# Two attention stages of a fused transformer kernel moved into the projection loop ahead of them

## The chip, the cores and the metric

The kernel runs on one core of one Trainium2 chip. The metric is the device time of one execution in microseconds; the median of several executions counts. Five engines work side by side and meet at semaphores: TensorE (PE, matrix products; PEld is its weight load), VectorE (DVE), ScalarE (ACT), GpSimd (POOL) and SyncE (SP). Here SP issues the weight loads and POOL a few small ones.

## The reference, cut to what matters

Two transformer blocks on 256 tokens of width 2048, all in float32. The change lies in the first block, between its first projection and its gated linear attention:

```
mod  = silu(c) @ w_ada + b_ada            # six rows of 2048, wanted later
h    = rms_norm(x) * (1 + scale1) + shift1
proj = h @ w_in                           # 7680 columns of q, k, v, r, then 16 of a, then the gates
o_sb  = stick_breaking_attention(rms_norm(q_sb), rms_norm(k_sb), v_sb)      # 6 heads of 128
o_dil = dilated_mixture(rms_norm(q_dil), rms_norm(k_dil), v_dil)            # 2 slots of 3 heads of 128
o_gla = gla_chunked(q_gla, k_gla, v_gla, log_sigmoid(a @ w_gla_a + b) / 16) # 4 heads
y = g0 * (o_sb @ w_br_sb) + g1 * (o_dil @ w_br_dil) + g2 * (o_gla @ w_br_gla)
```

A stick-breaking head needs, for 256 queries and keys: z = k q, softplus of z, its reverse running sum (a product with a triangle of -1), exp of z plus that sum under a strict causal mask, and the product with v. A dilated slot takes one softmax over the logits of three heads with a fixed bias each, and sums their products with v.

## The kernel before

**Products.** A weight tile of 256 x 512 (512 KB) lands in one of eight buffers `raw`. ACT copies it to `whi` in the rounded type float32r, DVE writes the rest of it to `wlo` (`split_item`, four buffers each), and PE makes 12 matmuls of 512 columns: high by high, low by high, high by low, for two halves of the tile and two blocks of tokens (`products`). Eight tiles make a group of 512 columns of `proj`; then ACT and DVE copy the two banks of the group to `proj1` (`proj1_evac`). The split of tile p + 4 waits for the product of tile p, so that up to three tiles lie ready when PE ends one.

**The stage of the first projection** (`ST_PROJ1`). The first three groups of columns are made while the modulation is computed. Then 96 tiles p = 0 to 95 follow in three rounds of 32, and between them 16 tiles of `w_ada` in each round, which DVE alone takes in (`ada_rows`, summed in `acc2`); at the end of each round PE turns that sum into columns (`ada_columns`). `BRANCH_ORDER` is the order of the 48 tiles of a round: four of the product, then one of `w_ada` and two of the product in turn. `drive` runs this order with an offset of four tiles. Behind the loop stands `side`, the 16 columns of a. The loads run up to eight tiles ahead of the splits; each waits until DVE has used up its buffer.

**Stages.** `stage_end` drains each of PE, ACT and DVE and makes them wait for each other. Behind the projection come the stage of the six stick-breaking heads (`ST_SB`), that of the dilated heads (`ST_DIL`) and that of the gated linear attention (`ST_GLA`). In the first two no weight tile is split or loaded beyond the eight that lie ready. `qk_norm` squares q and k of both kinds (ACT, `SQ1`), sums them, takes the root and multiplies. A head is a chain: PE turns q and k, DVE copies them out scaled (`qkt_evac`), PE makes z, ACT takes four functions of it, DVE adds and masks three times, PE makes the running sum, DVE adds and masks three times, ACT takes the exponential, PE multiplies with v, ACT and DVE copy out high and low part. Two heads are under way at once, in pairs of banks. POOL fetches the constants of each stage when the stage before it has ended (`wait_stage`).

Of the kernel before, what the change touches and what calls it, by code (L numbers as in the profile page):

```python
# [12 lines left out]
P = 128  # L13
# [83 lines left out]
def program(nc, I, out):  # L97
    ctx = ExitStack()
    with ctx:
# [15 lines left out]
        alo = sb("alo", [P, DC, TB * P], F32R)  # L115
        bhi = sb("bhi", [P, DC, TB * P], F32R)
# [5 lines left out]
        def pair_tile(t):  # L122

            pair = raw[:, t % 8 - t % 2:t % 8 - t % 2 + 2].rearrange("p h a (b n) -> p h (a b) n", n=HID)
            return pair[:, :, 2 * (t % 2):2 * (t % 2) + 2].rearrange("p h k n -> p k h n")

# [47 lines left out]
        class Chain:  # L174
# [11 lines left out]
        (ST_LOAD, ST_PROJ1, ST_SB, ST_DIL, ST_GLA, ST_BRANCH, ST_OUT1, ST_FFN, ST_PROJ2, ST_FOX, ST_OUT2,  # L186
         ST_MOE) = range(1, 13)
# [101 lines left out]
        moe_pe, moe_act, moe_dve = S("moe_pe"), S("moe_act"), S("moe_dve")  # L289

# [169 lines left out]
        side_t = {1: region(xf, 1280, 256), 2: region(big, T2, 256), 3: region(big, 5376, 256)}  # L460
# [3 lines left out]
        def _(pool):  # L464
# [12 lines left out]
            wait_stage(pool, ST_DIL)  # L477
# [28 lines left out]
        acc2 = region(xf, 256, 2 * COLS)  # L506
# [123 lines left out]
        def _(pe):  # L630
# [53 lines left out]
            def side(n, no, bias=None):  # L684
# [10 lines left out]
                ins.then_inc(S("side_mm"), 1)  # L695
                pe.wait_ge(S("side_t"), no)
# [3 lines left out]
                ins.then_inc(S("side_done"), 1)  # L700

# [60 lines left out]
            def proj1_tile(k, g, par):  # L762
                is_product, j = BRANCH_ORDER[k]
                if is_product:
                    q = j // 8
                    if j % 8 == 0:
                        group_free(g * 4 + (n_proj1 + q))
                    products(t_proj1 + k, g * 6, [(ahi, alo, 2 * (j % 8)), (ahi, alo, 2 * (j % 8) + 1)],
                             (2 * (q % 2), 2 * (q % 2) + 1), j % 8 == 0, j % 8 == 7, j)

            def proj1_ada(g, par):
                ada_columns(g * 48 + (t_proj1 + 48), g + 4, acc2, 5)
            drive(pe, 3, 48, proj1_tile, {47: proj1_ada}, single=True)
            side(16, 1)
            stage_end(pe, "pe")


            H = SB_HEADS
            pe.wait_ge(S("qk_scaled"), 1)
            for i in range(H + 3):  # L780
                if i < H:
                    qk_transposes("sb", i, i)
                h = i - 1
                if 0 <= h < H:
                    pe.wait_ge(S("sb_qkt"), 2 * (h + 1))
                    if h >= 2:
                        pe.wait_ge(S("sb_sp"), h - 1)
                    q, k = qkt_sb[:, h % 2, 0], qkt_sb[:, h % 2, 1]
                    mm(bank[2 + h % 2][:, 0:256], k[:, 0:P], q[:, 0:256], start=True, stop=True)
                    mm(bank[2 + h % 2][:, 256:384], k[:, P:256], q[:, P:256], start=True, stop=True)\  # L790
                        .then_inc(S("sb_z"), 1)
                h = i - 2
                if 0 <= h < H:
                    pe.wait_ge(S("sb_spm"), h + 1)
                    if h >= 2:
                        pe.wait_ge(S("sb_e"), h - 1)
                    sp_, C = l_sb[:, h % 2], bank[4 + h % 2]
                    mm(C[:, 0:P], negtri, sp_[:, 0:P], start=True, stop=True)
                    mm(C[:, P:256], negtri, sp_[:, P:256], start=True, stop=False)
                    mm(C[:, P:256], negones, sp_[:, 256:384], start=False, stop=True)  # L800
                    mm(C[:, 256:384], negtri, sp_[:, 256:384], start=True, stop=True).then_inc(S("sb_c"), 1)
                h = i - 3
                if 0 <= h < H:
                    pe.wait_ge(S("sb_w"), h + 1)
                    if h >= 2:
                        pe.wait_ge(S("sb_out"), h - 1)
                    _, _, _, v = att_cols("sb", h)
                    W, O = z_sb[:, h % 2], bank[6 + h % 2]
                    mm(O[:, 0:P], proj1[:, 0, v:v + DH], W[:, 0:P], start=True, stop=True)
                    mm(O[:, P:256], proj1[:, 0, v:v + DH], W[:, P:256], start=True, stop=False)  # L810
                    mm(O[:, P:256], proj1[:, 1, v:v + DH], W[:, 256:384], start=False, stop=True).then_inc(S("sb_o"), 1)
            stage_end(pe, "pe")

            def pv(kind, u, i):
                a = ATT[kind]
                per, n = a["per"], u * a["per"] + i
                pe.wait_ge(S(att(kind) + "_pt"), HEAD0[kind] + n + 1)
                if i == 0 and u >= 2:
                    pe.wait_ge(S(att(kind) + "_out"), UNIT0[kind] + u - 1)
# [8 lines left out]
            def attention(kind):  # L828
# [6 lines left out]
                for n in range(U * per + 2):  # L835
                    if n + 1 < U * per:
                        qk_transposes(kind, a["head"](*divmod(n + 1, per)), n + 1)
# [1609 lines left out]
```

## Time and profile before

| | us |
|---|---|
| median of 3 runs | 3216.33 (3214.28 to 3217.31) |
| the profiled execution | 3211.53 |
| its span in the trace | 3209.8 |
| PE, DVE, ACT busy in the span | 2909.0, 1979.2, 1480.1 |

The tiles of the projection's loop run from about 160 to 424 us of the span, the stick-breaking stage from 431 to 510, the dilated one to 544, and the gated linear attention to about 655. Times in the trace are counted from the start of the span. A matmul is listed with its latency, and several overlap; what one costs in a row of them is the distance from start to start. PEclk is the share of full clock that TensorE was granted: 0.5 is 1.2 GHz and 1.0 is 2.4 GHz, and a value between is a mean over a stretch.

### The profile page before, as it was taken

The page shows a single profiled execution, that of the slowest core. Times are in us where ns is not written, and L with a number is a line of the kernel's source. Part 1 is how long each engine was busy: PE and PEld are TensorE (multiplying, and loading weights), DVE is VectorE, ACT ScalarE, POOL GpSimd, SP SyncE. Part 2 cuts the span into 40 slices and gives each one's busy share as a digit, 9 for nine tenths or more (in the row PEclk, how much of TensorE's full clock was granted, in tenths as well). Part 3 has the DMA queues.
Part 4 walks back from the last instruction along what each step waited for, and adds up shares of the span by engine and source line. Part 5 has one row for each costly group of instructions (what it writes and reads, how often), then busy time and mean ns, then how long its engine had stood idle before and what let it go on. Part 6 is the DMA issues. An engine that isn't in the chain of part 4 may idle for free.

```text
span 3209.8 us, 38239 instructions
## 1 busy us (share of the span) xinstructions
PE 2909.0 (91%) x12771; PEld 2358.5 (73%) x12771; DVE 1979.2 (62%) x2206; ACT 1480.1 (46%) x1757; POOL 13.0 (0%) x21
## 2 busy tenths in 40 slices
PE   3799955799999899999999989977779999999989
PEld 3688853378887678888888868855668887878767
DVE  7876653367777744554555554446664557989875
ACT  3344343244444444444434444434354436777763
POOL 0000000000000000000000000000000000000000
PEclk8899976599999999999999999976889999999999
DMA  9988830078887746665665657710425568999964
GB/s 339 339 284 283 283 102 19 2 244 277 288 283 268 237 151 189 191 193 186 190 196 182 197 142 194 193 51 14 135 83 189 185 197 303 371 351 356 365 243 142
DMA packets 347283, 676.76 MB, mean 211 GB/s; under 512 B 23800, under 2 KB 114320, under 8 KB 346656
## 3 DMA queue, kind: packets, MB, share of 16 engines
q1 hardware_dynamic: 345664, 669.29, 63.2%
q0 software_dynamic: 1504, 5.95, 0.6%
q8 instruction: 72, 1.18, 0.2%
q14 instruction: 43, 0.35, 0.0%
HBM read 673.04 MB, written 2.10 MB: 210 GB/s over the span
## 4 chain that ended last, share of the span: by engine, by line
PE 75%; DVE 5%; ACT 3%; issue 1%; DMA 1%; DVEq 0%; ACTq 0%; POOL 0%; SPq 0%; POOLq 0%
PE bank L641 23%; PE bank L643 23%; PE bank L642 23%; PE bank L845 1%; PE bank L918 1%; ACT big L1222 0%; PE bank L848 0%; PE bank L1091 0%; DVE alo L1709 0%; PE bank L922 0%; DVE big L2212 0%; ACT whi L1206 0%; PE bank L920 0%; DVE big L2177 0%; DVE wlo L1683 0%
## 5 line engine op out<-in xcount | busy, mean ns | idle before, releaser
L641 PE MATMUL bank<-whi,ahi 128*128 128x512 f32 x2400 | 944.6, 394 | 43.2 <-DVE wlo L1873 30.2
L1671 DVE TENSOR_TENSOR wlo<-raw,whi 128x1024 fp32r<-128x1024 f32 x540 | 653.7, 1224 | 483.3 <-ACT whi L1200 478.7
L642 PE MATMUL bank<-wlo,ahi 128*128 128x512 f32 x2400 | 939.7, 392 | 0.0
L643 PE MATMUL bank<-whi,alo 128*128 128x512 f32 x2400 | 939.6, 392 | 0.0
L1200 ACT ACTIVATE whi<-raw 128x1024 fp32r<-128x1024 f32 x540 | 567.5, 1059 | 580.1 <-PE bank L643 524.9
L641 PEld LDWEIGHTS bank<-whi,ahi 128*128 128x128 f32 x2400 | 454.4, 189 | 139.1 <-issue 29.5
L643 PEld LDWEIGHTS bank<-whi,alo 128*128 128x128 f32 x2400 | 453.9, 189 | 96.1
L642 PEld LDWEIGHTS bank<-wlo,ahi 128*128 128x128 f32 x2400 | 454.5, 189 | 93.5
L1193 ACT ACTIVATE whi<-raw 128x1024 fp32r<-128x1024 f32 x280 | 296.7, 1061 | 432.2 <-PE bank L643 372.3
L1873 DVE TENSOR_TENSOR wlo<-raw,whi 128x1024 fp32r<-128x1024 f32 x280 | 341.8, 1224 | 205.9 <-ACT whi L1193 203.2
L641 PE MATMUL bank<-whi,bhi 128*128 128x512 f32 x944 | 369.8, 392 | 32.6 <-DVE wlo L1671 32.6
L642 PE MATMUL bank<-wlo,bhi 128*128 128x512 f32 x944 | 368.4, 390 | 0.0
L643 PE MATMUL bank<-whi,blo 128*128 128x512 f32 x944 | 368.3, 390 | 0.0
L1683 DVE TENSOR_TENSOR wlo<-raw,whi 128x1024 fp32r<-128x1024 f32 x256 | 302.1, 1222 | 69.0 <-ACT whi L1206 66.6
L1206 ACT ACTIVATE whi<-raw 128x1024 fp32r<-128x1024 f32 x256 | 262.6, 1056 | 90.0 <-PE bank L643 71.9
L641 PEld LDWEIGHTS bank<-whi,bhi 128*128 128x128 f32 x944 | 177.8, 188 | 70.9 <-issue 33.0
L643 PEld LDWEIGHTS bank<-whi,blo 128*128 128x128 f32 x944 | 177.8, 188 | 37.2
L642 PEld LDWEIGHTS bank<-wlo,bhi 128*128 128x128 f32 x944 | 177.9, 188 | 36.7
L641 PE MATMUL bank<-whi,ghi 128*128 128x512 f32 x384 | 154.2, 402 | 3.2 <-DVE wlo L1683 2.8
L643 PE MATMUL bank<-whi,glo 128*128 128x512 f32 x384 | 150.0, 391 | 0.0
L642 PE MATMUL bank<-wlo,ghi 128*128 128x512 f32 x384 | 149.8, 390 | 0.0
L1828 DVE SCALAR_TENSOR_TENSOR xres<-raw,silu_c,xres 128x1024 f32<-128x1024 f32 x105 | 134.8, 1284 | 9.7 <-ACT big L1447 4.4
(441 smaller groups left out, 1892.6 us busy)
## 6 DMA issues: line engine op xcount, KB each, us to landing
raw<-in_w_in SPq DMA_DIRECT2D x296, 512.0 KB, 4.6
raw<-in_w_ada SPq DMA_DIRECT2D x192, 512.0 KB, 5.3
raw<-in_w_ffn_in SPq DMA_DIRECT2D x352, 256.0 KB, 3.3
raw<-in_w_expert_gate SPq DMA_DIRECT2D x128, 512.0 KB, 5.6
raw<-in_w_expert_up SPq DMA_DIRECT2D x128, 512.0 KB, 6.5
raw<-in_w_expert_down SPq DMA_DIRECT2D x128, 512.0 KB, 6.2
raw<-in_w_ffn_out SPq DMA_DIRECT2D x88, 512.0 KB, 4.3
raw<-in_w_out SPq DMA_DIRECT2D x64, 512.0 KB, 4.6
```

The costliest lines, as they stand in the source:

```text
L641: mm(o, shi[:, kc, T], whi[:, s, c], start=st, stop=False)
L642: mm(o, shi[:, kc, T], wlo[:, s, c], start=False, stop=False)
L643: ins = mm(o, slo[:, kc, T], whi[:, s, c], start=False, stop=en)
L845: ins = mm(Z[:, zs], q[:, qs], k[:, ks], start=True, stop=not fox)
L918: mm(O, gl_sc[rows, h * 2 + b, :], proj1[rows, b, v:v + DV], start=True, stop=(c == 0))
L1193: A(whi[:, u % 4], raw[:, t % 8], ACT.Copy).then_inc(hi_ready, 1)
L1200: A(whi[:, t % 4], raw[:, t % 8], ACT.Copy).then_inc(hi_ready, 1)
L1206: A(whi[:, t % 4].rearrange("p k (h n) -> p k h n", h=2), pair_tile(t), ACT.Copy).then_inc(hi_ready, 1)
L1671: V.tensor_tensor(wlo[:, t % 4], raw[:, t % 8], whi[:, t % 4].bitcast(F32), ALU.subtract)\
L1683: V.tensor_tensor(as_tile(wlo[:, t % 4]), pair_tile(t), as_tile(whi[:, t % 4].bitcast(F32)), ALU.subtract).then_inc(lo_ready, 1)
L1828: V.scalar_tensor_tensor(sums, w, col, sums, ALU.mult, ALU.add).then_inc(lo_ready, 1)
L1873: V.tensor_tensor(wlo[:, u % 4], raw[:, t % 8], whi[:, u % 4].bitcast(F32), ALU.subtract)\
```

## The change

The two stages `ST_SB` and `ST_DIL` are gone. Their work is cut into slots, one for each tile p of the projection (`sb_step(h)` = 8 + 4h, `dil_step(u, i)` = 48 + 2(3u + i)). PE does its part of slot p right behind the product of tile p. ACT and DVE do theirs in `proj1_slot(p)`, which stands ahead of the split of tile p + 4. The norm of q and k is split in two, at p = 0 to 5 for the stick-breaking heads and at p = 40 to 45 for the dilated ones. The heads now have one bank for each purpose (4 for turned q and k and the columns of `w_ada`, 5 for z, 6 for the running sum or turned probabilities, 7 for the output) instead of pairs. `side_products` stands ahead of tile 0, its transposes behind tile 1. The sum of the `w_ada` rows lies in `acc1`, over the buffer of the attention outputs. POOL fetches the constants of the first kind when the normed x is there and the biases of the second when all six heads are out. The loop over the three rounds is written out.

```diff
-            wait_stage(pool, ST_PROJ1)
+            pool.wait_ge(S("norm_xn"), 2)
             fetch("sbc_landed", region(xf, X_SBC, 3 * P), I["consts"][:, C_U:C_U + 3 * P])
-            wait_stage(pool, ST_SB)
+            pool.wait_ge(S("sb_out"), SB_HEADS)
             for j in range(2):
                 fetch("dmask_landed", proj1[:, j, 0:3 * 384], I["consts"][:, at:at + 3 * 384])
-            wait_stage(pool, ST_DIL)
+            wait_stage(pool, ST_PROJ1)
             fetch("glac_landed", region(xf, G_R, 448), I["consts"][:, C_R:C_R + 448])
...
# PE
+            def sb_pe(p):
+                for h in range(SB_HEADS):
+                    at = p - sb_step(h)
+                    if at == 0:   # waits qk_scaled 1, sb_qkt 2h;        4 transposes -> bank 4, sb_T
+                    elif at == 2: # waits sb_qkt 2(h + 1), sb_sp h;      z -> bank 5 (256 + 128 columns), sb_z
+                    elif at == 5: # waits sb_spm h + 1, sb_e h;          running sum -> bank 6 (4 x 128), sb_c
+                    elif at == 7: # waits sb_w h + 1, v's group, sb_out h; output -> bank 7 (3 x 128), sb_o
+            def dil_pe(p):        # head n: transposes at 0, logits at 2; past 11 + i turned
+                                  # probabilities (3 x 128), past 12 + i the product with v (3 x 128)
+            side_products(16, 1)
+            for it in range(3):
+                for k, (is_product, j) in enumerate(BRANCH_ORDER):
+                    products(...)
+                    if p == 1:
+                        side_flip(16, 1)
+                    sb_pe(p)
+                    dil_pe(p)
+                    if j == 31:
+                        ada_columns(t_proj1 + 48 * (it + 1), it + 4, acc1, 4)
...
# ACT
+                    if at == 2:
+                        act.wait_ge(S("sb_z"), h + 1)
+                        A(ZS, Z, ACT.Copy).then_inc(S("sb_zs"), 1)
+                        chain.step(A(L, Z, ACT.Abs))
+                        chain.step(A(L, L, ACT.Exp, scale=-1.0))
+                        A(L, L, ACT.Ln, bias=1.0).then_inc(S("sb_ln"), 1)
+                    elif at == 6:
+                        act.wait_ge(S("sb_e"), h + 1)
+                        act.wait_ge(S("sb_em"), h + 1)
+                        A(ZS, ZS, ACT.Exp).then_inc(S("sb_w"), 1)
+                    elif at == 7:
+                        act.wait_ge(S("sb_o"), h + 1)
+                        A(bhi[:, h, :], bank[7][:, 0:256], ACT.Copy).then_inc(S("sb_ohi"), 1)
+            for p in range(96 + 4):
+                if p >= 4:
+                    proj1_slot(p - 4)
+                if p < 96:
+                    proj1_split(p)
+                else:
+                    branch_split(p - 96, 0, 0)
...
# DVE: at 0 q and k out of bank 4; at 3 (waits sb_ln) add, mask, mask; at 5 (waits sb_c, sb_zs)
# add, mask, mask; at 7 (waits sb_ohi) the low part of the output
+            for p in range(96 + 4):
+                if p >= 4:
+                    proj1_slot(p - 4)
+                if p < 96:
+                    split_item(t_proj1 + 48 * (p // 32) + item(p % 32), 0, u_proj1 + p, 0)
...
+                if p < 96:
+                    for k in range(item(p % 32) + 1, 48):
+                        if BRANCH_ORDER[k][0]:
+                            break
+                        ada_rows(t_proj1 + 48 * (p // 32) + k, 0, BRANCH_ORDER[k][1], acc1)
```

In ACT's stream of the kernel before, one head in the middle of the stick-breaking stage (the table loads are written by the compiler; L1385 is the exponential of the head before, L1377 to L1380 the four functions of this one):

```order
L1385 ACT_TABLE_LOAD
L1385 ACTIVATE xres<-xres 128x384
L1377 ACTIVATE xres<-bank 128x384
L1378 ACTIVATE xres<-bank 128x384
L1379 ACTIVATE xres<-xres 128x384
L1380 ACT_TABLE_LOAD
L1380 ACTIVATE xres<-xres 128x384
```

The same in the changed kernel, inside the projection (L1270 is the split, L1427 and L1420 to L1423 are the functions, L1430 copies the output):

```order
L1270 ACTIVATE whi<-raw 128x1024 x3
L1427 ACT_TABLE_LOAD
L1427 ACTIVATE xres<-xres 128x384
L1420 ACTIVATE xres<-bank 128x384
L1421 ACTIVATE xres<-bank 128x384
L1422 ACTIVATE xres<-xres 128x384
L1423 ACT_TABLE_LOAD
L1423 ACTIVATE xres<-xres 128x384
L1270 ACTIVATE whi<-raw 128x1024
L1430 ACTIVATE bhi<-bank 128x256
```

The functions and their two table loads are the same; four splits now stand in their round, one of them right behind the logarithm. DVE's stream before, in the same stage (L1949 to L1952 are the first add and its masks, L1755 takes q and k out of the bank, L1958 to L1961 are the second add and its masks):

```order
L1949 SCALAR_TENSOR_TENSOR xres<-bank,xres 128x384
L1951 TENSOR_TENSOR xres<-xres 128x128
L1952 TENSOR_TENSOR xres<-xres 128x128
L1755 TENSOR_SCALAR xres<-bank,vec 128x256 x2
L1949 SCALAR_TENSOR_TENSOR xres<-bank,xres 128x384
L1951 TENSOR_TENSOR xres<-xres 128x128
L1952 TENSOR_TENSOR xres<-xres 128x128
L1958 TENSOR_TENSOR xres<-xres,bank 128x384
L1960 TENSOR_TENSOR xres<-xres 128x128
L1961 TENSOR_TENSOR xres<-xres 128x128
```

And now, from the low part of one head's output (L1866) to the second add of the next head (L1979 is the split, L1934 a row of `w_ada`, L2013 takes q and k out, L2024 and L2031 are the two adds):

```order
L1979 TENSOR_TENSOR wlo<-raw,whi 128x1024
L1866 TENSOR_TENSOR blo<-bank,bhi 128x256
L2024 SCALAR_TENSOR_TENSOR xres<-bank,xres 128x384
L2026 TENSOR_TENSOR xres<-xres 128x128
L2027 TENSOR_TENSOR xres<-xres 128x128
L1979 TENSOR_TENSOR wlo<-raw,whi 128x1024
L1934 SCALAR_TENSOR_TENSOR acc_2497<-raw,silu_c,acc_2497 128x1024
L2013 TENSOR_SCALAR xres<-bank,vec 128x256 x2
L1979 TENSOR_TENSOR wlo<-raw,whi 128x1024
L2031 TENSOR_TENSOR xres<-xres,bank 128x384
L2033 TENSOR_TENSOR xres<-xres 128x128
L2034 TENSOR_TENSOR xres<-xres 128x128
```

Two splits and one row of `w_ada` now lie between the first and the second add of a head.

## Rows read from the trace of the kernel before

**Rows 1.** The page's first part: busy us (share of the span) xinstructions of TensorE.

```profile
PE 2909.0 (91%) x12771; PEld 2358.5 (73%) x12771; DVE 1979.2 (62%) x2206; ACT 1480.1 (46%) x1757; POOL 13.0 (0%) x21
```

**Rows 2.** Windows by stage: length, PE, PEld, DVE, ACT, POOL busy, PEclk, DMA share, GB/s.

```profile
166.00:423.00 257.00, 257.00 (x1154) 213.38 (x1152) 177.65 (x153) 104.25 (x105) 0.00 (x0) 1.00 0.88 286
431.00:450.00 19.00, 0.00 (x0) 0.00 (x0) 15.10 (x14) 6.06 (x5) 0.57 (x1) 0.55 0.04 10
450.00:509.00 59.00, 33.19 (x132) 28.11 (x132) 20.21 (x53) 32.94 (x49) 0.00 (x0) 0.59 0.00 1
509.00:544.00 35.00, 19.75 (x102) 16.70 (x102) 15.04 (x33) 6.85 (x16) 1.07 (x2) 0.72 0.10 34
```

**Rows 3.** Timeline of ScalarE in the projection's loop: start, length, then [idle before <-releaser].

```profile
163.42 1.06 ACT L1193 ACTIVATE whi<-raw 128x1024 fp32r<-128x1024 f32 x1 [1.65 <-PE bank L643]
```

**Rows 4.** Timelines at the projection's end: last tile's copy, `side` products, their transposes.

```profile
423.81 0.58 ACT L1329 ACTIVATE big<-bank 128x512 f32<-128x512 f32 x1
...
424.29 0.28 PE L690 MATMUL bank<-ahi,bhi 128*16 128x256 f32 x1
...
430.38 0.29 PE L698 MATMUL bank<-ident,xres 16*128 16x16 f32 x2 [0.46 <-ACT xres L1256]
```

**Rows 5.** Chain of waits from the dilated stage into the gated linear attention.

```profile
543.82 0.42 DVE blo L1760
...
548.20 0.60 PE bank L875 x2
```

**Rows 6.** Timeline of TensorE in the stick-breaking stage, at full clock.

```profile
453.62 0.60 PE L708 MATMUL bank<-ident,big 128*128 128x128 f32 x4
454.06 0.60 PE L789 MATMUL bank<-xres 128*128 128x256 f32 x2
454.50 0.38 PE L790 MATMUL bank<-xres 128*128 128x128 f32 x2
```

**Rows 7.** Timeline of ScalarE in the stick-breaking stage, one head.

```profile
496.90 0.49 ACT L1377 ACTIVATE xres<-bank 128x384 f32<-128x384 f32 x1 [1.51 <-issue]
...
497.81 0.52 ACT L1379 ACTIVATE xres<-xres 128x384 f32<-128x384 f32 x1
498.35 1.28 ACT L1380 ACT_TABLE_LOAD   x1
499.64 0.52 ACT L1380 ACTIVATE xres<-xres 128x384 f32<-128x384 f32 x1
...
502.60 1.28 ACT L1385 ACT_TABLE_LOAD   x1 [2.44 <-DVE xres L1961]
503.89 0.52 ACT L1385 ACTIVATE xres<-xres 128x384 f32<-128x384 f32 x1
```

**Rows 8.** Timeline of VectorE: two `w_ada` rows, split, copy, norm sums, heads.

```profile
414.39 2.68 DVE L1828 SCALAR_TENSOR_TENSOR xres<-raw,silu_c,xres 128x1024 f32<-128x1024 f32 x2
...
423.94 1.23 DVE L1873 TENSOR_TENSOR wlo<-raw,whi 128x1024 fp32r<-128x1024 f32 x1 [1.49 <-ACT whi L1193]
425.08 0.68 DVE L1886 COPY big<-bank 128x512 f32<-128x512 f32 x1
...
434.72 6.74 DVE L1728 TENSOR_REDUCE stat<-xres 128x12 f32<-128x1536 f32 x4
...
459.53 0.87 DVE L1755 TENSOR_SCALAR xres<-bank,vec 128x256 f32<-128x256 f32 x2
...
500.19 0.56 DVE L1949 SCALAR_TENSOR_TENSOR xres<-bank,xres 128x384 f32<-128x384 f32 x1 [4.35 <-ACT xres L1380]
...
501.32 0.55 DVE L1958 TENSOR_TENSOR xres<-xres,bank 128x384 f32<-128x384 f32 x1
```

**Rows 9.** Waits of TensorE from 2660 to 3060 us: total, times, longest.

```profile
PE bank L641 <- DVE wlo L1683: 2.8, 7, 1.0
```

**Rows 10.** DMA issues: a small fetch of POOL among loads, KB, us to landing.

```profile
big<-in_w_in POOLq DMA_DIRECT2D x1, 128.0 KB, 7.8
```

More of the change, by code:

```diff
@@ L769, in proj1_tile @@
                              (2 * (q % 2), 2 * (q % 2) + 1), j % 8 == 0, j % 8 == 7, j)
[L771 to L819, printed above, removed]
-                src, _, _, v = att_cols(kind, a["head"](u, i))
-                T, O = a["pt"][:, n % 2], bank[6 + u % 2]
-                mm(O[:, 0:P], src[:, 0, v:v + DH], T[:, 0:P], start=(i == 0), stop=False, skip_group_check=True)
-                mm(O[:, P:256], src[:, 0, v:v + DH], T[:, P:256], start=False, stop=False, skip_group_check=True)
-                ins = mm(O[:, P:256], src[:, 1, v:v + DH], T[:, 256:384], start=False, stop=(i == per - 1),
-                         skip_group_check=True)
-                ins.then_inc(S(att(kind) + "_O"), 1)
@@ L1023, in _, with pv @@
             stage_end(pe, "pe")
+            def pv(kind, u, i):
+                a = ATT[kind]
+                per, n = a["per"], u * a["per"] + i
+                pe.wait_ge(S(att(kind) + "_pt"), HEAD0[kind] + n + 1)
+                if i == 0 and u >= 2:
+                    pe.wait_ge(S(att(kind) + "_out"), UNIT0[kind] + u - 1)
+                src, _, _, v = att_cols(kind, a["head"](u, i))
+                T, O = a["pt"][:, n % 2], bank[6 + u % 2]
+                mm(O[:, 0:P], src[:, 0, v:v + DH], T[:, 0:P], start=(i == 0), stop=False, skip_group_check=True)
+                mm(O[:, P:256], src[:, 0, v:v + DH], T[:, P:256], start=False, stop=False, skip_group_check=True)
+                ins = mm(O[:, P:256], src[:, 1, v:v + DH], T[:, 256:384], start=False, stop=(i == per - 1),
+                         skip_group_check=True)
+                ins.then_inc(S(att(kind) + "_O"), 1)
@@ new lines, in qk_norm_act @@
+            def qk_norm_act(p, first, no, col):
+                at = p - first
+                if at in (0, 1):
+                    last = group_of(col + 1535)
+                    act.wait_ge(evac_dve if at else evac_act, last + 3)
+                    A(SQ1[:, at], proj1[:, at, col:col + 1536], ACT.Square).then_inc(S("qk_sq"), 1)
+                elif at == 3:
+                    act.wait_ge(S("qk_var"), no + 1)
+                    A(stat[:, 16:40], stat[:, 16:40], ACT.Sqrt).then_inc(S("qk_std"), 1)
@@ new lines, in dil_act @@
+            def dil_act(p):
+                a = ATT["dil"]
+                for n in range(DIL_SLOTS * DIL_GROUPS):
+                    u, i = divmod(n, DIL_GROUPS)
+                    past = p - dil_step(u)
+                    if past == 8 and i == 0:
+                        act.wait_ge(S("att_max"), u + 1)
+                        L = a["logit"][:, u % 2]
+                        for qb, cols in ((0, slice(0, P)), (1, slice(P, 384))):
+                            j = (u % 2) * 2 + qb
+                            A(L[:, :, cols], L[:, :, cols], ACT.Exp, bias=stat[:, j:j + 1],
+                              accum_out=stat[:, 8 + j:9 + j]).then_inc(S("att_exp"), 1)
+                    elif past == 11 + i:
+                        act.wait_ge(S("att_PT"), n + 1)
+                        if n >= 2:
+                            act.wait_ge(S("att_O"), n - 1)
+                        A(a["pt"][:, n % 2], bank[6][:, 0:384], ACT.Copy).then_inc(S("att_pt"), 1)
+                    if past == 14 and i == 0:
+                        act.wait_ge(S("att_O"), DIL_GROUPS * (u + 1))
+                        A(bhi[:, a["dst"] + u, :], bank[7][:, 0:256], ACT.Copy).then_inc(S("att_ohi"), 1)
```

421 lines of the change are left out of this document (268 added, 153 removed).

## The prediction, made before the changed kernel ran

> **What bounds the kernel now.** I read the page first, then windows by stage, then timelines at the seams, and last the chain of waits. TensorE is busy 91% of the span [rows 1]; the question is where it is not. In the projection's loop it never pauses: busy 257.00 of 257 us at full clock, with the DMA engines at 0.88 and DVE at 177.65 / 257 = 69% [rows 2]. There ACT waits 1.65 us for the product ahead of each split of 1.06, so a step of one tile takes 2.71 us, and TensorE sets it [rows 3]. Behind it come 113 us in which TensorE does little and DMA almost nothing: none of PE while DVE sums and scales q and k, then 33.19 of 59 and 19.75 of 35, at a granted clock of 0.59 and 0.72 [rows 2]. These are chains of short steps: while ACT runs its functions, DVE and PE wait. The loop has room on ACT and DVE; the two stages have room everywhere. So a head that moves into the loop costs what it adds to TensorE, if ACT and DVE keep ahead.
>
> **What goes.** The last tile's copy starts at 423.81, `side` follows at 424.29 and its transposes at 430.38 [rows 4], and the gated linear attention starts on PE at 548.20 [rows 5]. From 423.81 to 548.20 are 124.4 us. Everything after 548.20 is unchanged, so the sum asks only when that instruction starts now.
>
> **What TensorE gains in work.** At full clock four transposes take 454.06 - 453.62 = 0.44 us, and 256 columns 0.44 more, so 128 columns of float32 take 0.22 [rows 6]. A stick-breaking head: transposes 0.44, z 384 columns 0.66, running sum 512 columns 0.88, output 384 columns 0.66, together 2.64. A dilated head: 0.44, logits 0.66, three transposes of probabilities 0.33, output 0.66, together 2.09. Six of each: 15.8 + 12.5 = 28.3 us. The same matmuls cost about twice this in the old stages wherever the clock was at its lower level. `side` keeps its cost of some 5.5 us (424.29 to 430.38, less ACT's copy and the wait) and moves to the front, where it delays tile 0 by as much; its copy and transposes, which stood on the path, are hidden there by three tiles that lie ready.
>
> **What ACT and DVE add to the path.** Average load first. In four steps PE needs 4 x 2.71 + 2.64 = 13.5 us. DVE has four splits of 1.23, two rows of `w_ada` of 1.3, q and k 0.87, two groups of three small operations of 1.2, the low part 0.42 and half a copy of 0.68: 11.6 us [rows 5, 8]. ACT has four splits of 1.06, 3.3 us from the copy of z to the end of the logarithm, 1.8 for the load and exponential, 0.4 for the output: 9.8 [rows 3, 7]. Both have room. But both work in order, and one round of waits passes through both. Begin when DVE ends the second add of head h (slot step 5). ACT: load and exponential 1.82, then the four functions of head h + 1, 3.29, then the split behind them, 1.06. DVE: that tile's low part 1.23, output low 0.42, first add and masks 1.13, then, as the order of its stream shows, split 1.23, `w_ada` row 1.3, q and k 0.87, split 1.23, and only then second add and masks 1.28 (501.32 to 502.60) [rows 5, 7, 8]. The sum is 14.9; back-to-back DVE operations overlap by some 0.1 each, which takes 0.4 off, and every second head has a copy of 0.68 in it, 0.34 on average: **14.8 us per head, against 13.5 on PE**. So PE must wait about 1.3 us per head, in front of the running sum and the output; six heads give **8 us**. The bounds are 0 (all slack absorbed by the tiles that lie ready, which this round doesn't allow) and 2 x 8. The norm at p = 0 to 5 is eight wide operations in all (half of them here) of 1.7 to 1.8 us on DVE (15.10 busy of 19 in that window, 6.74 for four sums) [rows 2, 8]: 7 us of work on top of 9 us of splits and rows in six steps of 2.71. That eats some 3 us of the 8 us that three ready tiles give; PE first asks for the result at p = 8. No cost. The same at 40 to 45, with a table load more on ACT, far from its limit. The dilated heads have 5.1 us of DVE work in two steps of PE, which take 5.4 + 1.1, and no round through ACT like the above: no cost. What hides all of this is the product of the loop; if it were not there, each head would cost its chain, as before.
>
> **Loads.** POOL's biases wait for all six outputs (p = 35) and are used at p = 50, over 40 us later; even the slowest small fetch of the trace, 7.8 us among loads [rows 10], fits five times. The first constants are fetched in the start-up, where the DMA engines are full: 192 KB, at the 286 GB/s of the loop 0.7 us at worst. The fetch for the gated linear attention now stands beside the last weight loads instead of an idle queue: between 0 and 5 us (7.8 less the 2 to 3 us of an idle one), and I take 1, since only one or two tiles are still under way. The loop written out adds no work.
>
> **The sum.** The last copy moves from 423.8 to 423.8 + 5.5 + 28.3 + 8 = 465.6. Behind it ACT copies 0.58 and splits 1.06, DVE splits 1.23, to 468.5. From DVE's last operation to the first transpose took 548.20 - 544.24 = 3.96 [rows 5]: 472.4. That is 75.8 us earlier; less 0.7 and 1 it is 74. The trace's 3209.8 would become 3136; the profiled execution, 3211.5, lies 4.8 below the median, so the median goes from 3216.3 to **3142 us**.
>
> **A rule against it.** In the old stage the exponential starts at 497.81, ends at 498.33, and the load starts at 498.35; the logarithm starts 0.01 behind the load's end [rows 7]. So a switch costs 1.28 us and nothing more. The Trainium skill, "ScalarE: Activation LUTs", section "What ACT_TABLE_LOAD costs", adds a drain of about 1380 ns to each load of 1283 ns. By that, an estimate from the page, each head would pay 2.8 us more on the round and six heads 17 us. The trace disagrees where a chain has already emptied the engine; behind a split of 1.06 us it shows nothing.
>
> **Rivals.** (a) *PE never waits.* The ready tiles and the overlap of small steps cover the round. For it: DVE is loaded to 86% only. Against: the order of its stream. 8 us less: 3134. (b) *The round is longer.* Each handover between engines, or each load behind a split, costs more than in the old stage. If every one of two loads per head cost once more its own 1.28 us, six heads pay 15 us: 3157. For it: the loads now stand behind splits; against it the rows just read. (c) *The loop starves the clock: slower.* While the heads ran alone, PE at 56% busy had 0.59 of the clock [rows 2]. If waits at the running sum brought the clock to its lower level in the loop too, a product would take 2.71 us more. It decides at 75 / 2.7 = 28 steps: with more of the 60 steps of p = 8 to 67 at the lower level the change loses. All 60 would give 163 us and the small matmuls 28 more: 3333. Against it: PE stays about 90% busy, and late in the kernel it waits up to 1.0 us for DVE [rows 9] in stretches whose granted clock is 1.00. (d) *It doesn't do what it says:* some wait on a single bank, or DMA running behind DVE's later splits, serializes the slots, at 10 us or more beyond (b): above 3166.
>
> **How the numbers follow.** Forecast 3142, meaning 3137 to 3150: 0.58. (a), 3129 to 3137: 0.16. (b), 3150 to 3166: 0.16. (d): 0.06. (c): 0.04. The range 3129 to 3166 leaves out (c), (d) and little else. Measurement can tell 0.2%, some 6 us. Only (c) can end slower: 0.04; nothing but a part of (c) or (d) lands within 0.2%: 0.01; faster 0.95.
>
> **What would show it.** Windows: no stretch between the projection and the gated linear attention with PE below half; loop length 264 + 5.5 + 28 + 8 us. Waits: PE in front of the running sum, released by DVE's mask, and in front of the output, released by ACT's exponential, about 1 us each from the second head on; none in the norm stretches, none among the dilated heads. ACT: four functions in 3.3 us, the load directly behind the split. Clock 1.00 throughout. I am wrong if PE waits in front of `products` for DVE's split, if a gap stands before a table load, or if heads come more than 16 us apart.

## The result and the profile after

The changed kernel takes 3137.98 us (median of 4 executions, 3137.61 to 3138.53) against 3215.62 of before in the same comparison: ratio 0.9758, 95% interval 0.9742 to 0.9775. That is 78 us less; forecast were 74 from 3216.3, which gave 3142 in a range of 3129 to 3166. The spans of the two profiled executions, 3209.8 and 3136.8, differ by 73.0. The other 5 us are a matter of which execution was profiled: that of before, 3211.53, lay 4.8 below its median, that of the changed kernel, 3138.53, 0.6 above its own.

The page first: its span and PE's line, which answers to [rows 1].

```profile
span 3136.8 us, 38049 instructions
PE 2887.6 (92%) x12771; PEld 2338.8 (75%) x12771; DVE 1975.6 (63%) x2208; ACT 1478.0 (47%) x1760; POOL 13.0 (0%) x21
```

The same 12771 matmuls are there. The kernel makes no fewer products; 73 us are gone from the path. The windows that answer to [rows 2]: the stretch of the stick-breaking heads, of the two norms' second half and the dilated heads, the rest of the loop, the seam behind it, and the gated linear attention (length, then PE, PEld, DVE, ACT, POOL busy, PEclk, DMA share, GB/s).

```profile
190.00:280.00 90.00, 87.32 (x437) 71.22 (x436) 64.20 (x91) 56.79 (x75) 0.00 (x0) 1.00 0.71 222
280.00:370.00 90.00, 90.00 (x434) 75.40 (x433) 78.36 (x90) 42.23 (x48) 1.07 (x2) 1.00 0.84 281
370.00:455.00 85.00, 85.00 (x401) 71.01 (x400) 57.87 (x54) 35.94 (x43) 0.00 (x0) 1.00 0.81 261
455.00:475.00 20.00, 13.58 (x70) 11.49 (x69) 10.08 (x10) 5.79 (x6) 1.53 (x3) 0.92 0.82 271
475.00:556.00 81.00, 61.43 (x159) 23.55 (x160) 19.71 (x45) 26.98 (x48) 0.00 (x0) 0.56 0.00 0
```

There is no longer a stretch with PE under half between the projection and the gated linear attention. ACT went from 41% (104.25 of 257) to 63% (56.79 of 90) in the head stretch, and DVE from 69% to 87% in the dilated one (78.36 of 90), while PE stays at 97 to 100% and at full clock. Only the last row, with a granted clock of 0.56, is like the old stages with their 0.59 and 0.72.

One round of a head, ScalarE (start, length, instruction, and in brackets the idle time before it and who ended it), which answers to [rows 3, 7]:

```profile
226.81 1.28 ACT L1427 ACT_TABLE_LOAD   x1 [4.94 <-DVE xres L2034]
228.11 0.53 ACT L1427 ACTIVATE xres<-xres 128x384 f32<-128x384 f32 x1
228.54 0.47 ACT L1420 ACTIVATE xres<-bank 128x384 f32<-128x384 f32 x1
228.91 0.48 ACT L1421 ACTIVATE xres<-bank 128x384 f32<-128x384 f32 x1
229.42 0.53 ACT L1422 ACTIVATE xres<-xres 128x384 f32<-128x384 f32 x1
229.96 1.28 ACT L1423 ACT_TABLE_LOAD   x1
231.26 0.53 ACT L1423 ACTIVATE xres<-xres 128x384 f32<-128x384 f32 x1
231.69 1.04 ACT L1270 ACTIVATE whi<-raw 128x1024 fp32r<-128x1024 f32 x1
...
241.08 1.28 ACT L1427 ACT_TABLE_LOAD   x1 [4.34 <-DVE xres L2034]
```

and VectorE in the same round, from one second mask (L2034) to the next, which answers to [rows 8]:

```profile
226.44 0.29 DVE L2034 TENSOR_TENSOR xres<-xres 128x128 f32<-128x128 f32 x1
...
232.76 1.23 DVE L1979 TENSOR_TENSOR wlo<-raw,whi 128x1024 fp32r<-128x1024 f32 x1 [3.50 <-ACT whi L1270]
233.90 0.42 DVE L1866 TENSOR_TENSOR blo<-bank,bhi 128x256 fp32r<-128x256 f32 x1
234.24 0.55 DVE L2024 SCALAR_TENSOR_TENSOR xres<-bank,xres 128x384 f32<-128x384 f32 x1
...
235.36 1.22 DVE L1979 TENSOR_TENSOR wlo<-raw,whi 128x1024 fp32r<-128x1024 f32 x1
236.68 1.28 DVE L1934 SCALAR_TENSOR_TENSOR acc<-raw,silu_c,acc 128x1024 f32<-128x1024 f32 x1
237.88 0.87 DVE L2013 TENSOR_SCALAR xres<-bank,vec 128x256 f32<-128x256 f32 x2
238.67 1.22 DVE L1979 TENSOR_TENSOR wlo<-raw,whi 128x1024 fp32r<-128x1024 f32 x1
239.80 0.55 DVE L2031 TENSOR_TENSOR xres<-xres,bank 128x384 f32<-128x384 f32 x1
...
240.71 0.29 DVE L2034 TENSOR_TENSOR xres<-xres 128x128 f32<-128x128 f32 x1
```

This is the round of the prediction, read from top to bottom across the two: the mask at 226.44 ends ACT's idle time, ACT goes from 226.81 to 232.73 without a gap through load, five functions, load and split, that split ends DVE's idle time of 3.50, and DVE goes from 232.76 to 241.00 without a gap. The two stand idle in turn, at 63% and 71% busy in this stretch, and neither is a bottleneck by its busy share. The distances of the six masks L2034 are 14.87, 14.27, 14.87, 15.65 and 13.4 us (in the fourth there is a second row of `w_ada`; in the fifth ACT has no functions of a next head).

What TensorE waited for between 190 and 466 us (total, times, longest):

```profile
PE bank L817 <- DVE xres L2027: 1.0, 2, 0.5
PE bank L811 <- DVE xres L2013: 0.8, 1, 0.8
PE bank L826 <- ACT xres L1427: 0.5, 1, 0.5
```

L817 is the running sum, L811 is z, L826 the output (the wait in front of z, in the fourth round, was not forecast). 2.3 us are listed. A matmul's listed end lies after the point at which the next could start (0.39 long, 0.23 apart), so the list shows only what goes beyond that; distances between copies of groups, below, give the whole.

Last the seam, as the chain of waits gives it, which answers to [rows 5]:

```profile
466.89 1.69 PE bank L758 x16
468.77 1.19 DVEq L168
470.04 0.51 issue
470.54 1.04 POOL xres L485 x2
471.58 3.28 DMA xres<-in_b_gla_a
474.99 0.60 PE bank L898 x2
```

L898 is the first matmul of the gated linear attention. It was at 548.20 [rows 5] and is at 474.99 now, 73.2 us earlier, and the spans differ by 73.0: behind it the two traces add up to the same within 0.2.

### The profile page after: what moved, and what is told of

Its sections match the earlier page's. It is cut to its first block, busy times and chain, and to the rows that moved or that the text cites. A ratio compares the mean times of both kernels' runs of the same rounds, so it can differ in the third digit from the quotient of the medians.

```text
span 3136.8 us, 38049 instructions
## 1 busy us (share of the span) xinstructions
PE 2887.6 (92%) x12771; PEld 2338.8 (75%) x12771; DVE 1975.6 (63%) x2208; ACT 1478.0 (47%) x1760; POOL 13.0 (0%) x21
## 4 chain that ended last, share of the span: by engine, by line
PE 84%; DVE 9%; ACT 3%; issue 2%; DMA 1%; DVEq 0%; ACTq 0%; POOL 0%; SPq 0%; POOLq 0%
PE bank L660 26%; PE bank L661 25%; PE bank L662 25%; DVE big L1934 2%; DVE wlo L1979 1%; PE bank L941 1%; PE bank L758 0%; ACT big L1299 0%; PE bank L1083 0%; PE bank L1168 0%; DVE alo L1817 0%; PE bank L945 0%; DVE big L2373 0%; PE bank L943 0%; PE bank L1080 0%
## 5 line engine op out<-in xcount | busy, mean ns | idle before, releaser
L1270 ACT ACTIVATE whi<-raw 128x1024 fp32r<-128x1024 f32 x280 | 295.5, 1060 | 360.3 <-PE bank L662 300.7
L1979 DVE TENSOR_TENSOR wlo<-raw,whi 128x1024 fp32r<-128x1024 f32 x280 | 341.3, 1223 | 194.3 <-ACT whi L1270 191.1
L1934 DVE SCALAR_TENSOR_TENSOR big<-raw,silu_c,big 128x1024 f32<-128x1024 f32 x75 | 96.3, 1284 | 7.1 <-DMA raw<-in_w_ada 0.5
```

Of the source, the lines that this page charges most:

```text
L1270: A(whi[:, u % 4], raw[:, t % 8], ACT.Copy).then_inc(hi_ready, 1)
L1934: V.scalar_tensor_tensor(sums, w, col, sums, ALU.mult, ALU.add).then_inc(lo_ready, 1)
L1979: V.tensor_tensor(wlo[:, u % 4], raw[:, t % 8], whi[:, u % 4].bitcast(F32), ALU.subtract)\
```

## The experiments

To measure the loop I take the copies of the 12 groups of columns (ACT L1457; L1329 before), which stand at p = 7, 15, ... 95. The six stick-breaking heads lie between p = 7 and 39, the dilated ones behind that (with heads five tiles apart the last one reaches past 39, so there only the whole loop compares). The first column is the time of the copy at p = 7, the next three are distances, all in us. The copy starts 0.43 behind the group's last matmul on PE, but 1.45 behind it in before and with the slot behind the split, where ACT makes a split first; in these two rows the first column is 1.0 too late against the others and the last one 1.0 too short.

| | p = 7 | p = 7 to 39 | p = 7 to 95 | last copy to L898 | median us |
|---|---|---|---|---|---|
| before | 180.71 | 88.88 | 243.10 | | 3214.5 to 3215.7 |
| after | 189.16 | 110.52 | 277.77 | 8.06 | 3137.98 |
| no table loads | 187.57 | 105.54 | 272.81 | 8.02 | 3130.48 (3128.84 to 3134.19) |
| two more loads a head | 188.16 | 125.66 | | | 3149.54 (3149.05 to 3153.54) |
| slot behind the split | 187.51 | 112.07 | 279.32 | 6.70 | 3138.47 (3135.64 to 3140.19) |
| heads every five tiles | 187.90 | 106.39 | 274.60 | 7.95 | 3134.04 (3132.68 to 3134.81) |
| first fetch later | 189.27 | 110.50 | 277.75 | 7.90 | 3138.17 (3137.32 to 3139.82) |
| last fetch earlier | 187.65 | 110.51 | 277.76 | 3.13 | 3128.86 (3127.74 to 3134.61) |
| the three edits together | 187.43 | 106.34 | 274.58 | 3.13 | 3126.94 (3124.08 to 3129.57) |
| after, repeated | 187.70 | 112.11 | 279.36 | 7.91 | 3138.25 (3135.82 to 3139.20) |
| last fetch earlier, repeated | 187.84 | 110.48 | 277.73 | 3.13 | 3127.35 (3126.69 to 3131.21) |
| that and five tiles | 188.97 | 106.35 | 274.59 | 3.13 | 3122.92 (3122.50 to 3125.32) |

### Is it the round, and do the table loads set it?

Without the loads: the logarithm is replaced by an exponential, which needs no other table.

```diff
-                        A(L, L, ACT.Ln, bias=1.0).then_inc(S("sb_ln"), 1)
+                        A(L, L, ACT.Exp, bias=1.0).then_inc(S("sb_ln"), 1)
```

> The changed kernel with the logarithm of each stick-breaking head replaced by an exponential, so that ACT needs no table load per head (the heads' values are wrong by that; every instruction but the loads stays). Theory of the round (em of head h, ACT's exponential and four functions, split, DVE's low part and first add, two splits and a w_ada row, second add: 14.3 to 15.7 us per head in the trace against 13.5 of PE work): two loads of 1.28 less make the round 12.3, PE sets the pace, heads come 13.3 to 13.7 us apart, the waits of PE at the running sum and the output vanish, and the time falls by 6 to 7 us to about 3132. Rival (the loop's excess is the price of small matmuls between the products, and the round is covered): no change, 3138.

Measured: the head stretch shrinks from 110.52 to 105.54, and between 190 and 466 us PE waits for nothing that is listed. The window over the heads is full, with ACT at 52% instead of 63%:

```profile
190.00:280.00 90.00, 90.00 (x463) 76.26 (x462) 70.30 (x100) 46.62 (x66) 0.00 (x0) 1.00 0.75 240
```

So 105.54 - 88.88 = 16.7 us is what six heads cost TensorE in work, and 5.0 us is what they cost in waits; the rest of the stretch behind p = 39 is unchanged (167.25 of after, 167.27 here). The median fell by 7.5 and the traced span by 9.8, more than 5.0: this trace is also 1.6 earlier at p = 7, and 2.7 shorter between 926 and 2122 us, where nothing was edited. The runs further down take up both.

The opposite: two more loads in each head, by a logarithm of one column behind the exponential.

```diff
                         A(ZS, ZS, ACT.Exp).then_inc(S("sb_w"), 1)
+                        A(stat[:, 63:64], ones[:, 0:1], ACT.Ln, bias=1.0)
```

> The changed kernel with one more logarithm of a single column behind each head's last exponential, which costs ACT two more table loads per head. Round theory: the round grows by 2 x 1.28 + 0.2 = 2.8 us, heads come 17.1 to 18 us apart, and five passes of the round add 14 us: 3152. Rival (the tiles that lie ready and idle time of ACT cover it): ACT is busy 9.8 of 14.8 us per head, so up to 5 us more would fit in, and the time stays within 3 us of 3138.

Measured: PE's waits between 190 and 466 us, and ACT's stream from a head's exponential to the third function of the next head (the first two stand at the dots), now with a load on each side of the added logarithm:

```profile
PE bank L817 <- DVE xres L2028: 11.7, 5, 3.3
```

```profile
246.97 0.52 ACT L1427 ACTIVATE xres<-xres 128x384 f32<-128x384 f32 x1
247.51 1.28 ACT L1428 ACT_TABLE_LOAD   x1
248.81 0.20 ACT L1428 ACTIVATE stat<-ones 128x1 f32<-128x1 f32 x1
...
249.79 1.28 ACT L1422 ACT_TABLE_LOAD   x1
251.08 0.52 ACT L1422 ACTIVATE xres<-xres 128x384 f32<-128x384 f32 x1
```

The heads now come 17.67, 17.06, 17.66, 18.46 and 16.2 us apart, 2.8 more than before this edit each time: two loads of 1.28 and one function of 0.2. The head stretch is 15.1 us longer and the span 15.0. Five distances of 2.8 are 14.0 of it: all of ACT's added time reaches the end, though ACT is busy for 65% of the window (58.38 of 90). The other 1.1 stand behind the sixth head's mask, where most of a product runs at the lower level of the clock. In this trace the clock falls to it three times in the loop, from 223.7, 257.8 and 295.4 us, for 3 to 4 us each, at the end of a wait at the running sum of 3.31, 3.33 and 2.07 us or within 1.5 us behind it (two waits of 1.5 have no such dip). The second:

```profile
257.75 0.76 PE L817 MATMUL bank<-xres 128*128 128x128 f32 x2 [3.33 <-DVE xres L2028]
258.31 0.63 PE L818 MATMUL bank<-xres 128*128 128x128 f32 x2
```

The distances show nothing of the first two dips, since PE waits in the round anyway; behind the last head nothing covers the third. The round sets the pace; taking 2.56 us from it frees only 1 us per head, because then PE's own work is the longest: without the loads the heads come 13.65 us apart in the mean. (The medians differ by 11.6, less than the 14 forecast and than the traces: the profiled execution, 3153.54, was the slowest of its four.)

### Can the same round be hidden by order or by distance?

The slot behind the split instead of ahead of it, on both engines:

```diff
             for p in range(96 + 4):
-                if p >= 4:
-                    proj1_slot(p - 4)
                 if p < 96:
                     proj1_split(p)
                 else:
                     branch_split(p - 96, 0, 0)
+                if p >= 4:
+                    proj1_slot(p - 4)
```

> The changed kernel with ACT's and DVE's slot of step p - 4 behind the split of tile p instead of ahead of it, nothing else. Round theory: going through the streams, the round holds the same pieces (exponential, four functions, one split on ACT; three splits, one w_ada row, q and k, low part, two adds on DVE), 14.9 us, so the time stays: 3138 within 2 us. Rival (the place ahead of the split is what makes the heads fit): every handover to PE comes one split later, 2.3 us, twice per head, PE waits at the running sum and at the output, and the time grows by 12 us or more.

Measured: 3138.47 against 3137.98, no difference. The stretch is 1.55 longer, with a clock of 0.54 from 273 to 276 us and of 0.90 to 279, a dip that the repeated run of the unedited kernel shows as well (below); the seam is 1.4 shorter, of which 1.0 is only the later copy. The round holds the same pieces either way: ACT's part one split, DVE's part three and one row of `w_ada`. The first three distances of the masks are 14.67, 14.07 and 14.68. The words of the change, "ahead of the split", decide nothing here.

Five tiles between heads instead of four, so that 13.5 us of PE become 16.2. The round grows less: on ACT a split now lies between the exponential and the next head's functions, and the first masks come 16.46 and 15.68 apart instead of 14.87 and 14.27 (the dilated norm at p = 41 and heads from p = 50 on; two waits for banks adapted):

```diff
-            return 8 + 4 * h
+            return 8 + 5 * h
-        SB_NORM, DIL_NORM, DIL_FIRST = 0, 40, 48
+        SB_NORM, DIL_NORM, DIL_FIRST = 0, 41, 50
```

> The changed kernel with the stick-breaking heads five tiles apart instead of four (and the dilated part one or two steps later). Round theory: the round gains one split, 1.2, and half a w_ada row, 0.65, to 16.7 us, PE's own period one product, 2.7, to 16.2 to 16.4: the excess per head falls from 1.2 to 0.4 and the time by 4 to 5 us, to about 3134. Rival (small matmuls cost what they cost): no change, 3138.

Measured: p = 7 to 95 takes 274.60, 3.2 less than after, and the median falls by 3.9 to 3134.04. The window over the heads, to compare with 87.32 of after and 90.00 without loads:

```profile
190.00:280.00 90.00, 89.00 (x448) 74.77 (x447) 68.44 (x94) 56.20 (x70) 0.00 (x0) 1.00 0.76 242
```

Two thirds of the wait go without any work being taken away: a longer distance gives PE more work than it adds to the round. 1.8 us remain against the kernel without loads (272.81). One wait is listed in this loop, 1.0 us at 262.46 in front of the fourth head's output, released by ACT's exponential; where the rest stands isn't listed.

### Small fetches at both ends

The tile 0 of the loop came later than forecast, so POOL's first fetch was moved behind the first three groups of columns:

```diff
-            pool.wait_ge(S("norm_xn"), 2)
+            pool.wait_ge(evac_act, 5)
```

> The changed kernel with POOL's first fetch (192 KB of constants) issued when the first three groups of columns are copied out, at about 163 us of the span, instead of when the normed x is there, at 35 us, where the DMA engines are full. They are used at p = 6, some 25 us later. Theory (the early fetch pushes the weight loads of the start-up back, which are its bound): tile 0 comes 2 to 3 us earlier and the time falls to 3135 to 3136. Rival (the 3.3 us by which the start-up is longer in the changed kernel's trace are scatter between executions, and the fetch costs its 0.5 us): within 1 us of 3138.

Measured: 3138.17, and p = 7 at 189.27 against 189.16. Nothing; the theory is wrong and the rival right. In all rows of the table but that of before the p = 7 copy lies between 187.4 and 189.3, without relation to the edits, and in two traces of the same kernel at 189.16 and 187.70: the start-up scatters by some 2 us (by PE's last matmul of that tile, which leaves out where the copy stands, 186.1 to 188.9 in the eleven traces with the change).

The last fetch doesn't need the end of the stage, only the last dilated output:

```diff
-            wait_stage(pool, ST_PROJ1)
+            pool.wait_ge(S("att_out"), DIL_SLOTS)
             fetch("glac_landed", region(xf, G_R, 448), I["consts"][:, C_R:C_R + 448])
```

> The changed kernel with the constants of the gated linear attention fetched when both dilated outputs are written (p = 68) instead of at the end of the projection's stage. Theory: the 6.4 us that PE waits for that fetch in front of the attention are late next, and with it gone PE starts when DVE's last split and the drains are through, 1 to 2 us behind the last split: 4.4 to 5 us less, 3133 to 3134. Rival (the pause is the split and the drain, and the fetch is hidden in it, or its transfer now delays the weight loads by as much): 3137 to 3138.

Measured: POOL issues it at 393.20 instead of 470.54, and the median is 3128.86, 9.1 us below after, nearly twice the 4.9 that the seam gives (8.06 down to 3.13 from last copy to L898) and more than either theory had. The three edits together:

> e_five, e_late and e_glac together. If the three causes are apart from each other (round of the heads 4, start-up 0.5 to 3, fetch ahead of the gated linear attention 4.5), the time is 3138 less 9 to 11.5: 3126.5 to 3129. If they share a cause (weight loads behind all of them), less than 7 is gained: above 3131.

3126.94, as forecast for three separate causes, though one of the three, the first fetch, gives nothing by itself. To see whether the other 4 us of the fetch belong to the edit, the unedited kernel, the earlier fetch, and the fetch with heads every five tiles ran again side by side, five times each.

> The changed kernel once more, nothing edited, beside the two below. Both theories: a median between 3137 and 3139. What it tells is how far two executions of the same program lie apart stage by stage: if scatter accounts for what the earlier fetch seemed to give beyond 4.9 us, the last copy of the projection and the way from the gated linear attention to 2130 us of the span differ between this trace and the first one by 1 to 3 us, though the code is the same.

> The fetch for the gated linear attention waits for the last dilated output instead of the end of the stage; the same kernel as the first run of this edit, repeated for more executions. Theory: only the wait of 5 us behind the last copy goes; the rest of the first run's 9.1 us was scatter in the start-up (1.5) and in products between 934 and 2132 us (2.5). Then the median lies 4 to 6 us below the repeated changed kernel: 3132 to 3134. Rival: the fetch also frees something later, and the gain is 8 to 10 us again: 3128 to 3130.

> The same edit together with heads every five tiles; POOL's first fetch is left as in the changed kernel. Theory: the two gains add, 4 to 6 us from the fetch and 3 to 5 from PE no longer waiting in the round, so 7 to 11 us below the repeated changed kernel: 3127 to 3131, and no different from the version that moved the first fetch too (3126.9), because that one only looked different by scatter. Rival: the first fetch does cost 3 us of start-up, and this version lies 3 us above that one, at 3130 or more.

Measured: 3138.25, 3127.35 and 3122.92. The gain of the fetch is 10.9 us, where the theory had 4 to 6 and the rival 8 to 10: it is no chance of one execution. The spans, 3136.4 and 3124.9, differ by 11.5; the traces give its places. Seam and start of the gated linear attention in the repeated kernel and in the one with the earlier fetch:

```profile
474.97 0.58 PE L898 MATMUL bank<-ident,gl_a 128*16 128x128 f32 x2 [6.27 <-DMA xres<-in_b_gla_a]
476.10 2.07 PE L902 MATMUL bank<-xres 16*128 16x512 f32 x2 [0.55 <-ACT xres L1505]
```

```profile
468.70 0.38 PE L898 MATMUL bank<-ident,gl_a 128*16 128x128 f32 x2 [1.49 <-DVEq L168]
469.62 1.48 PE L902 MATMUL bank<-xres 16*128 16x512 f32 x2 [0.55 <-ACT xres L1505]
```

4.8 us are the wait. 0.7 us follow from it: L898 and L902 still run at full clock behind an idle time of 1.49, and at the lower level behind 6.27 (0.38 against 0.58, 1.48 against 2.07). The other 6 us are in places that the edit doesn't touch, and in all that could be located the clock stood at its other level in the same instructions. In the repeated kernel, in the loop itself, right behind a wait of 0.46 and the sixteen one-column matmuls of `ada_columns`:

```profile
272.79 1.84 PE L758 MATMUL bank<-ones,acc 128*128 128x1 f32 x16
274.50 0.63 PE L660 MATMUL bank<-whi,ahi 128*128 128x512 f32 x1
...
277.91 0.48 PE L662 MATMUL bank<-whi,alo 128*128 128x512 f32 x1
278.23 0.39 PE L660 MATMUL bank<-whi,ahi 128*128 128x512 f32 x1
```

These products stand 0.43 apart instead of 0.23, and the stretch p = 7 to 39 takes 112.11 instead of 110.52. The first trace of the same kernel has no such dip, nor has that of the earlier fetch; the one with the slot behind the split has. And late in the kernel, in an attention stage whose heads are chains of short matmuls at the lower level, one head (25 matmuls) of the repeated kernel and the same head with the earlier fetch, as windows:

```profile
2107.00:2115.30 8.30, 8.06 (x25) 5.72 (x25) 3.27 (x11) 1.41 (x7) 0.00 (x0) 0.50 0.00 0
```

```profile
2098.00:2104.30 6.30, 6.07 (x25) 4.76 (x25) 3.31 (x12) 1.42 (x6) 0.00 (x0) 0.70 0.00 0
```

2.0 us in one head, because the clock was up for a part of it: in the trace of the repeated kernel this head's copies L1356 stand at 2106.62 and 2115.26, 8.64 apart, in the other at 2097.67 and 2104.33, 6.66 apart. By places: loop 1.5, seam 4.8, start of the gated linear attention and its end 0.7 and 1.0, a thin stretch near 1080 us 0.6, this head 2.0 with 0.5 around it, 0.4 elsewhere, together 11.5. That an earlier arrival decides which instructions meet the full clock is what these pairs suggest; no run shows it by itself, so of the 10.9 us only the wait and what follows at once from it, 5.5, are shown to be the fetch's. The three traces with this fetch and the early first one take 1195.4 to 1195.5 us (and the kernel without loads 1195.4) from the stage end near 926 to 934 us to the one near 2120 to 2130; after, its repetition, the later first fetch, five tiles, the slot behind the split and the three edits together take 1198.0 to 1198.6, before 1198.5. The kernel with two more loads takes 1198.1. Why a kernel falls into the one group or the other was not found.

The last of the three, with both edits, is the fastest that ran: 3122.92 us, ratio 0.9717 to before (0.9703 to 0.9730) and 15.3 us below the repeated changed kernel, more than the 7 to 11 forecast and than the 8 us that its waits account for (4.8 and 3.2). Moving the first fetch as well, in the run of the three edits together, came out 4 us slower, and in the traces 3.1 of 4.3 lie in the stretch of 1198.5; that the two would be alike, as the theory had it, did not hold.

## The prediction, point by point

**What bounds the kernel, and what goes.** Right. The loop held the heads at the price of TensorE's work and some waits; 124.4 us of path went, and L898 came 73.2 earlier, forecast 75.8 less 1.7 for the two fetches. In the old stages PE was busy for 33.19 + 19.75 = 52.9 us with the heads, at a granted clock of 0.59 and 0.72 [rows 2]; in the loop they add 29.7 of work. The rest of the old stages' time was waiting.

**TensorE's added work.** 15.8 forecast for the stick-breaking heads, 16.7 measured; 12.5 for the dilated ones, 13.0 measured (p = 39 to 95, 167.25 against 154.22). The small matmuls themselves are right or cheaper, but the product behind them takes 2.82 to 2.86 us instead of 2.72, which the sum by columns [rows 6] left out. Its first matmul takes 0.31 to the next instead of 0.23; whether the change from float32 to float32r makes that, no run separates.

**The round.** 14.8 us forecast, 14.87, 14.27 and 14.87 measured in the undisturbed heads, by the order of instructions given. PE's own 13.5 were 13.65. The mis-sized term is the wait that follows: 8 us was 1.3 times six, but six heads have five distances, and the difference is 1.0 in each. That gives the 5.0 measured. Rival (a), PE never waits, is refuted by 5 us, and its number, 3134, is what the run with heads every five tiles gave. Rival (b) did not come true. Its arithmetic is right, though: the kernel with two more loads has the longer round that the rival assumed, and its head stretch grew by 15.1 us, of which 14.0 by the round, where the rival had 15.

**The loads' price.** Sized right, 1.28 each, and the case that stood open is settled. Behind a split in the changed kernel:

```profile
347.54 1.05 ACT L1270 ACTIVATE whi<-raw 128x1024 fp32r<-128x1024 f32 x1
348.61 1.28 ACT L1442 ACT_TABLE_LOAD   x1
349.91 0.62 ACT L1442 ACTIVATE xres<-xres,stat 128x384 f32<-128x384 f32 x1
```

0.02 us before the load and 0.02 behind it, so no drain as the Trainium skill ("ScalarE: Activation LUTs", "What ACT_TABLE_LOAD costs") adds to each switch. The run that added two loads agrees (the one without loads cannot tell, since PE's own work then sets the pace): 2.8 us for two loads and a small function, where that rule would ask for about 5.5, an estimate from the page's figures.

**The front.** 5.5 for `side` and 0.7 for the fetch, 6.2 together. By its last matmul on PE the tile p = 7 came 9.4 us later in the first trace and 8.0 in the repeated one (188.73 and 187.27, before 179.31); its copies say 8.45 and 7.0, since before's stood further behind PE. From the last matmul of the start-up's groups to that of p = 7 it takes 27.84 us in both traces, against 21.76 before: `side` costs 6.1. The other 3.3 and 1.9 stand ahead of it (160.89 and 159.43, before 157.55); 2.2 and 1.8 of them are there at the first product of the last six tiles of the start-up (142.13 and 141.70, before 139.93). The run with the later fetch shows that the fetch is not the cause. The eleven traces with the change have that last matmul at 158.2 to 161.0; of before there is one trace, so whether its 157.55 is scatter is not shown.

**The seam.** Forecast from last copy to L898 6.8 us (465.6 to 472.4) and 1 more for the fetch; measured 8.06. The forecast took over that the copy stands 1.45 behind PE; from PE's last product it had 9.2 and measured are 8.5. From the end of DVE's last operation, the split of 1.22 at 468.69, to L898 it is 5.1, forecast 3.96 [rows 5] and 1. Right in size, but the prediction took these 5 us as given. They are a wait in the wrong place: POOL starts only when all engines have left the stage, and the fetch then takes 3.28. Issued 77 us earlier it costs nothing.

**The clock.** Rival (c) was given 0.04 and a price of 2.7 us for each product at the lower level. In the first trace it is at 1.00 throughout the loop; in the repeated one it shows once, for some 4 us, at a price of 1.6, with 12 matmuls at 0.43 instead of 0.23 apart 2.4 a product. With two more loads a head it shows three times, at waits of 2 to 3 us at the running sum, as the rival described it, and 1.1 us of that reach the end. The mechanism exists in this loop, at about a fiftieth of the 75 us from which it would decide. **Everything behind L898** was called unchanged. By structure that holds; by time it does not hold within 3 us, since identical code gained or lost this much when it was reached at another moment.

**The number.** The forecast for the trace was 3136, measured 3136.8, and that is closer than its terms are. In the first trace the front was 3.2 us longer than the sum had it and TensorE's work 1.5, while the waits of the round were 3.0 and the seam 0.8 shorter: most of it cancels, and that part is luck. The median, forecast 3142, came 4 us lower, since the sum added 4.8 for the distance of before's profiled execution from its median, and the changed kernel's had no such distance.

## What to carry to other kernels

When a serial chain is laid into a full loop, compare the loop engine's work per item with the longest round of waits through the in-order queues of the helpers, each with whatever stands between, not with their busy shares; if the round is longer, put the items further apart before making the steps cheaper. Then look at what the move brought to the end: a fetch that waits for a whole stage should wait for the last user of its buffer. A gain read off one stage of a trace and a gain of the whole can differ by several us where the clock has two levels, so look for the difference in later stages that the edit didn't touch before giving it to the edit.

## What the runs showed of the hardware

- TensorE's clock can drop inside a stream of products. It did so behind sixteen one-column matmuls and a wait of 0.46 us, for some 4 us, in two of the seven traces that have such a wait there, and three times in the trace with two more loads, at waits of 2.07 to 3.33 us, but not at two waits of 1.5.
- Whether a thin stage gets the full clock for a part of its time changed with the time of its arrival, worth 2.0 us in one head, and 3 us over 1200 us of unedited code.
- ACT can load a table while its instruction still waits: a load of 1.28 stood at 308.98, and the root it belongs to started at 311.10, when DVE's sum had come. Ahead of the heads' exponential it doesn't: that load stands behind the wait of 4.94, inside the round.
